# A row of RMS factors: made by TensorE transposes, or by a write to DRAM and a broadcast read

## The reference

```python
def rmsnorm(x, g):
    return x * lax.rsqrt(jnp.mean(x * x, axis=-1, keepdims=True) + EPS) * g

x = x + mixed @ w_o                      # mixed: gated sum of a convolution and a windowed attention
h2 = rmsnorm(x, mlp_norm_g)
x = x + jnp.square(jax.nn.relu(h2 @ w_up)) @ w_down      # w_up 1024x4096, w_down 4096x1024
return rmsnorm(x, final_norm_g)
```

## Time and profile before

| | |
|---|---|
| median of 3 runs | 763.24 us (763.02 to 763.28) |
| profiled execution | 763.45 us, of which the span from the first to the last instruction is 761.7 us |
| TensorE (matmul) busy | 752.7 us, 99% of the span |
| VectorE busy | 637.4 us, 84% |
| ScalarE busy | 407.6 us, 54% |
| GpSimd busy | 75.9 us, 10% |
| DMA | 128.13 MB, mean 168 GB/s |
| granted TensorE clock | 0.998 of full |

### The profile page before, as it was taken

The page is one execution under the profiler, slowest core; times in us unless marked ns, Lnnn a source line. Parts: engine busy times, 40 slices in busy tenths (PEclk is TensorE's granted clock), DMA queues, the critical chain, the costliest instruction groups (busy, mean ns, idle before and its releaser), DMA issues.

```text
span 761.7 us, 11518 instructions
## 1 busy us (share of the span) xinstructions
PE 752.7 (99%) x4563; PEld 675.0 (89%) x4563; DVE 637.4 (84%) x752; ACT 407.6 (54%) x529; POOL 75.9 (10%) x113
## 2 busy tenths in 40 slices
PE   8999999999999999999999999999999999999996
PEld 7888888888888999999988899889998999899985
DVE  5766688889896979886869899998799869986997
ACT  7424554453644655636616786654555356445565
POOL 3201000101112001010010101010101000010102
PEclk9999999999999999999999999999999999999999
DMA  7727313131219876779736866777676767777702
GB/s 255 244 83 278 111 55 111 56 111 55 72 39 262 242 186 169 194 237 327 235 80 198 219 160 173 174 205 177 175 209 172 215 166 190 196 184 203 194 1 111
DMA packets 70451, 128.13 MB, mean 168 GB/s; under 512 B 2620, under 2 KB 26244, under 8 KB 70404
## 3 DMA queue, kind: packets, MB, share of 16 engines
q1 hardware_dynamic: 53040, 85.23, 33.8%
q0 software_dynamic: 17152, 41.96, 25.4%
q10 hardware_dynamic: 212, 0.28, 0.1%
HBM read 121.14 MB, written 6.32 MB: 167 GB/s over the span
## 4 chain that ended last, share of the span: by engine, by line
PE 97%; DVE 1%; DMA 1%; ACT 0%; issue 0%; SPq 0%; ACTq 0%; DVEq 0%
PE pair L848 37%; PE pair L875 24%; PE pair L651 10%; PE pair L653 10%; PE pair L652 10%; PE pair L698 2%; PE pair L673 1%; PE pair L672 1%; PE pair L682 1%; DMA xn<-in_x 1%; PE pair L744 1%; PE pair L746 0%; PE pair L745 0%; PE pair L800 0%; DVE home_lo L1698 0%
## 5 line engine op out<-in xcount | busy, mean ns | idle before, releaser
L1164 ACT ACTIVATE high<-home_raw 128x2048 fp32r<-128x2048 f32 x84 | 160.9, 1916 | 156.2 <-PE pair L848 88.7
L1698 DVE TENSOR_TENSOR home_lo<-home_raw,high 128x2048 fp32r<-128x2048 f32 x84 | 192.2, 2288 | 35.3 <-ACT high L1164 34.7
L651 PE MATMUL pair<-h,wgt 128*128 128x512 f32 x320 | 126.7, 396 | 0.0
L653 PE MATMUL pair<-h,wgt 128*128 128x512 f32 x320 | 124.9, 390 | 0.0
L652 PE MATMUL pair<-h,wgt 128*128 128x512 f32 x320 | 124.8, 390 | 0.0
L653 PEld LDWEIGHTS pair<-h,wgt 128*128 128x128 f32 x320 | 60.1, 188 | 13.0
L652 PEld LDWEIGHTS pair<-h,wgt 128*128 128x128 f32 x320 | 60.3, 188 | 11.5
L651 PEld LDWEIGHTS pair<-h,wgt 128*128 128x128 f32 x320 | 60.2, 188 | 11.5
L875 PE MATMUL pair<-high,s_hi_tile 128*128 128x512 f32 x280 | 70.1, 391 | 0.0
L875 PE MATMUL pair<-home_lo,s_hi_tile 128*128 128x512 f32 x280 | 69.7, 390 | 0.0
L875 PE MATMUL pair<-high,s_lo_tile 128*128 128x512 f32 x280 | 69.7, 389 | 0.0
(11 more groups left out here) (222 smaller groups left out, 1151.8 us busy)
## 6 DMA issues: line engine op xcount, KB each, us to landing
raw<-in_w_in SPq DMA_DIRECT2D x42, 512.0 KB, 4.8
home_raw<-in_w_up SPq DMA_DIRECT2D x16, 1024.0 KB, 5.5
home_raw<-in_w_down SPq DMA_DIRECT2D x16, 1024.0 KB, 5.1
home_raw<-in_w_up POOLq DMA_DIRECT2D x12, 1024.0 KB, 8.4
home_raw<-in_w_down POOLq DMA_DIRECT2D x12, 1024.0 KB, 8.5
home_raw<-in_w_conv_out SPq DMA_DIRECT2D x4, 1024.0 KB, 8.2
home_raw<-in_w_attn_out SPq DMA_DIRECT2D x4, 1024.0 KB, 5.2
home_raw<-in_w_in SPq DMA_DIRECT2D x4, 1024.0 KB, 5.4
```

Source lines behind the costliest of these rows:

```text
L651: mm(bank[j][:, :], wh, rhs[:, 0, k, :], start=(k == 0), stop=False)
L653: last = mm(bank[j][:, :], wl, rhs[:, 0, k, :], start=False, stop=(k == KT - 1))
L1164: a(high[n % 2][:, :], home_raw[home_of(s, name)][:, :], ACT.Copy).then_inc(m_hi, 1)
L1698: v.tensor_tensor(home_lo[home][:, :], home_raw[home][:, :], f32(high[n % 2][:, :]), ALU.subtract).then_inc(m_lo, 1)
```

## The change

- VectorE no longer copies the factors to `rbc`, and TensorE no longer transposes it. PSUM bank 7 isn't used for this, and the wait of product N2 in stage 5 is gone.
- The reciprocals `rr2[:, 1, :]` are written to a tensor in DRAM, `factors_row`, by a DMA on ScalarE's queue: 128 partitions with 4 values each, so 128 pieces of 16 bytes. ScalarE waits until this has landed and then issues the read: 512 values, 2 KB, to each of 128 partitions, in the tile `rraw`. In memory the order is token-in-block first, block second, so ScalarE's copy from `rraw` to `rrow` puts it in order by reading with a stride of 4 values.
- `token_sums` stands one place earlier in VectorE's list, ahead of `low_part(4, M6)`, and `token_factors` ahead of `h2_low(M5)`. The root on ScalarE stands ahead of `high_part(4, M5)`. The write is issued behind that, the read behind `h2_high(M7)`.
- POOL waits for the read (`rrow_in`) before it issues the adding load T3 of stage 5.

```diff
@@ POOL
             for s in range(STAGES):
+                if s == 5:
+                    pool.wait_ge(rrow_in, 16)
                 pool.wait_ge(b12_in, 16 * (s + 1))
                 pool.dma_start(home_rows(home_of(s, "T3")), weights(s, 1, 1), accum_op=ALU.add).then_inc(t3_in, 16)
@@ PE
-            def row_transposes():
-                pe.wait_ge(rbc_ready, 1)
-                pe.wait_ge(h2_raw, 12)
-                for b in range(TB):
-                    last = nc.tensor.transpose(bank[7][:, b * P:(b + 1) * P], rbc[:, b, :], ident[:, :])
-                last.then_inc(rrow_t, 1)
...
-                    up_product(s, M5, True, between=(0, row_transposes) if s == 4 else None)
+                    up_product(s, M5, True)
...
-                if s == 5:
-                    pe.wait_ge(rrow_ready, 1)
                 product(s, N2, s < 6)
@@ ACT
                     h2_high(M5)
+                    act.wait_ge(rr2_step, 1)
+                    a(rr2[:, 0, :], ss2[:, 2, :], ACT.Sqrt, bias=eps[:, :], scale=1.0 / D).then_inc(rr2_step, 1)
                 high_part(s, M5)
                 if first:
-                    act.wait_ge(rr2_step, 1)
-                    a(rr2[:, 0, :], ss2[:, 2, :], ACT.Sqrt, bias=eps[:, :], scale=1.0 / D).then_inc(rr2_step, 1)
-                if first:
+                    act.wait_ge(rr2_step, 3)
+                    act.dma_start(factors_row[:, :], rr2[:, 1, :]).then_inc(row_out, 16)
                     h2_high(M7)
+                    act.wait_ge(row_out, 16)
+                    act.dma_start(rraw[:, :], bass.AP(factors_row[:, :].tensor, 0, [[0, P], [1, T]])).then_inc(rrow_in, 16)
                 else:
                     square(s, 0)
                 high_part(s, M7)
                 copy_out(s, zc12, M6, -1.0)
                 if first:
-                    act.wait_ge(rrow_t, 1)
-                    a(rrow[:, :], bank[7], ACT.Copy).then_inc(rrow_ready, 1)
+                    act.wait_ge(rrow_in, 16)
+                    a(rrow[:, :].rearrange("p (b n) -> p b n", b=TB), rraw[:, :].rearrange("p (n b) -> p b n", b=TB),
+                      ACT.Copy).then_inc(rrow_ready, 1)
@@ DVE
                 v.reciprocal(rr2[:, 1, :], rr2[:, 0, :]).then_inc(rr2_step, 1)
-                dve.wait_ge(rr2_step, 3)
-                v.tensor_copy(rbc[:, :, :], rr2[:, 1, :].rearrange("p (b n) -> p b n", n=1).to_broadcast([P, TB, P])
-                              ).then_inc(rbc_ready, 1)
...
             h2_low(M6)
+            token_sums()
             low_part(4, M6)
-            token_sums()
+            token_factors()
             h2_low(M5)
-            token_factors()
             low_part(4, M5)
```

More of the change, by code:

```diff
@@ L239, in build @@
         ty = place("ty", [P, 2, T])
-        rbc = place("rbc", [P, TB, P], offset=ty_at + 4 * T)
         zc11, zc12, zc22 = (place(n, [P, 4, 2 * P], offset=o) for n, o in
@@ L277, in build @@
         rrow = place("rrow", [P, T], offset=rrow_at)
+        rraw = place("rraw", [P, T], offset=ty_at + 4 * T)
         vdif = place("vdif", [P, TB - 1, KV * HD], offset=rrow_at)
@@ L295, in build @@
         h_sums = nc.dram_tensor("h_sums", (4, 2, P, 8 * P), F32)
+        factors_row = nc.dram_tensor("factors_row", (P, TB), F32)
         pair = [ctx.enter_context(nc.psum_tensor(f"pair{i}", [P, 2, T], F32)) for i in range(4)]
@@ L338, in build @@
         h2_sums, h2_split, h2_ready = sem("h2_sums"), sem("h2_split"), sem("h2_ready")
-        ss2_ready, rr2_step, rbc_ready = sem("ss2_ready"), sem("rr2_step"), sem("rbc_ready")
-        rrow_t, rrow_ready = sem("rrow_t"), sem("rrow_ready")
+        ss2_ready, rr2_step = sem("ss2_ready"), sem("rr2_step")
+        row_out, rrow_in, rrow_ready = sem("row_out"), sem("rrow_in"), sem("rrow_ready")
         b11_in, b22_in = sem("b11_in"), sem("b22_in")
```

## The result

The changed kernel takes 767.67 us (median of 6 runs, 766.73 to 768.82), the kernel before 763.05 us on the same chip (762.71 to 763.28). The ratio is 1.0061, with a 95% interval of 1.0050 to 1.0071: slower by 4.6 us, where 1.0 was predicted, and 0.8 us above the range.

The account below looks back on a forecast made before the run. TensorE, 97% of the chain, was taken to bound the kernel. T2's lateness of 1.67 less 0.66 slack gave +1.01, swallowing the 0.44 gain; 761.7 + 1.01 + 1.75 = 764.46, adjusted to the median: 764.2 us, range 762.6 to 766.9.

Parts of the forecast that it names:

- TensorE's gain: Four transposes of the broadcast factors leave TensorE's chain with nothing replacing them: -0.44 us by themselves.
- VectorE's and ScalarE's lists: Moved sums, reciprocal and root cause no stall; ScalarE's 2.08 us idle covers the write's wait; strided copy stays near 0.59 us.
- The row's time: Write to DRAM lands in 2.8 us, read in 2.6 us; the row is in SBUF at 461.1 us.
- my upper bound of 3.1: Longest landing allowed for the row's read: 2.5 us fixed plus 0.64 for 0.26 MB.
- the row's own bounds: Row in SBUF between 459.7 and 462.9 us, from the bounds of write and read.
- The estimate that the prediction works out from the Trainium skill: Each transfer about 2.0 us fixed plus bytes at 436 GB/s; both 4.6 us, row at about 460.3.
- The adding load: T3 (B22 added to B12, stage 5) issued 3.0 us late, lands in 8.3; VectorE's sum T2 starts 1.67 us late.
- the sign of sharing: T3 landing more than 9 us after its issue would show it sharing the DMA engines.
- rival 2: T3 shares DMA engines with SyncE's B21 load, taking 2.6 us more; TensorE loses 3.6 us: 766.9 us; chance 0.12.
- The slack: Least slack in VectorE's late queue is 0.66 us, at sum s1 of stage 5; TensorE's end moves +1.01 us.
- Rival 3: Write 3.9 us, read 3.1; row at 462.9, T3 at 471.45, TensorE +2.8: 766.0 us; chance 0.24 including cases down to +1.5.

Follow-up runs that it names:

- e8: Kernel before without the four transposes of the broadcast factors and without ScalarE's wait for them (factors not the tokens'): 762.55 us against 763.02.
- e5: Kernel before, with T3 of stage 5 also waiting for ScalarE's conversion of M7's weights in stage 4, no row transfer: 764.34 us against 763.02.
- e3: Changed kernel, with SyncE's load of B21 for stage 5 issued only when T3 has landed: 766.87 us against 763.11.
- e2: Kernel before, with only T3 of stage 5 made to wait, for rrow, and no transfer of a row: 768.06 us against 763.11.
- e13: Changed kernel without GpSimd's wait, SyncE issuing the 16-byte write and the read behind B21, first relu, square and rounding of stage 4 later: 765.59 us.
- e4: Changed kernel with 28 unused transposes of the identity matrix filling TensorE's gap in M3 of stage 4: 767.33 us against 763.11.
- e10: Changed kernel, the read taking 128 different 2 KB pieces of another DRAM tensor (factors not the tokens'): 767.82 us against 763.26.
- e1: Changed kernel without GpSimd's wait for the row's read ahead of T3: 764.53 us against 763.11.

## Why the prediction was wrong

**TensorE's gain.** 0.44 us, right: e8 measured 0.47, with the interval given above.

**VectorE's and ScalarE's lists.** Right. token_sums, the root, the reciprocal and the first relu came without a stall of note, and ScalarE's 1.97 us of idle time before M7's conversion hid the wait for the write. The copy's time doubled, where I had chosen no change; it hid too. The stride is the likely reason, and not SBUF: the squaring pass of ScalarE over 128x512 values in SBUF, without a stride, takes 0.63 us (line 1301 of before).

**The row's time.** The write was right, 2.8 us. The read was mis-sized: 3.7 us against 2.6, outside my upper bound of 3.1. The row came at about 462.0 in the times of before and not at 461.1, still inside the row's own bounds (459.7 to 462.9). The fault lies in the read's upper bound: I had added up a fixed part from large loads and the bytes at full rate, with nothing for packets that all read one place or for a slow start behind the small write. The estimate that the prediction works out from the Trainium skill (DMA: Bandwidth & Descriptors, Anatomy of one DMA), 4.6 us for both transfers, was further off: they took 6.5. The 256 KB stores' 2.1 us, which I said agree with it, are 0.5 us under the 2.6 that it gives for them.

**The adding load.** That it waits, that VectorE waits for it and what is queued behind, was right. Its duration is the step that failed: 8.3 us assumed, 10.3 measured, beyond the 9 us that I had named as the sign of sharing. I took 8.3 us from before, and set sharing with B21 (rival 2) aside for two stage 6 rows, from which I read "the one that moves first goes first". What they showed was only that a plain load starts late behind an adding one. B21, issued at 463.96 in after, moved its first packets after 467.5, and then took every second packet. In e5 T3 was issued 1.2 us earlier than in after, B21 started at the same point, T3 had nearly finished by then, and T3 took 8.6 us. The rule of the Trainium skill (DMA: Bandwidth & Descriptors, Queues, rings and completion order), round-robin between the queues with work, agrees with the 16 and 16 packets above; where I placed it beside the stage 6 rows, it was right and I was not. When a queue's first packets come is another matter, and that is what the stage 6 rows showed. Sharing is 0.9 us of T3's excess (after against e3, 10.3 and 9.4). The other 1.1 us are the one late part of T3's 16; that the fetch of instructions makes it late is likely and not shown.

**The slack.** The number 0.66 us at s1 was right where the lateness was 1.68 us (e5). At 4.57 us it would still be the place that costs most, 4.57 - 0.66 = 3.9 us, if the clock held. But the gap then comes first at an earlier place, the remainder of M3's weights. Its slack is 1.78 us (before: written by 472.57, read from 474.35), less the 0.44 us by which TensorE is early: 4.57 - 1.78 + 0.44 = 3.2 us of lateness, as measured. The fall of the clock behind this gap adds 1.59 and so brings TensorE past s1: 4.57 - 1.78 + 1.59 = 4.4 us. The prediction didn't count with the clock at all; it put that term at nothing.

**The miss in parts.** The row's lateness alone (T3 issued at 462.26, landing in 8.3 us) would have given 765.2 us by the prediction's own sum, inside the range. T3's further 2.0 us make it 767.2, the clock's share beyond s1, 4.4 - 3.9, some 767.6; measured were 767.67.

**The rivals.** Rival 2, with a chance of 0.12, named the mechanism and the place, and its 766.9 us are near the measured 767.7. That its figure is so near is luck in part: it took 2.6 us of sharing with the row on time, while sharing measured 0.9 and the late row, the late part of T3 and the clock made up the rest. Rival 3 named the slow read, together with a slow write that didn't come. The row came 0.9 us sooner than it said (462.0 against 462.9) and T3 still landed 1.1 us later (472.5 against 471.45). The effects add: a read 1.1 us late moves T3 into B21's time and that of the fetch. I had priced them one at a time.

## What to carry to other kernels

A wait put on a queue of loads costs what the delayed load then meets, and not the delay alone: price the load in its new place, against the transfers of that time, and ask when the next queue's packets come. When a gap on TensorE becomes likely, add what the clock takes behind it, and look for the next slack that this uses up. An instruction that fills another's wait isn't free to be moved, even when its own result is needed late.

## What was not expected of the hardware

A plain 1 MB load issued 2.3 us behind an adding one landed in 10.0 us instead of 5.0. One of the 16 parts of a transfer landed about 1.0 us behind the other fifteen (0.96 us in after, 1.06 in e3, 1.13 in e2), and the transfer with it. A write of 2 KB in 512 pieces of 4 bytes landed in 8.7 and 10.0 us, with some 5 us in which no DMA engine showed work and nothing landed; in 128 pieces of 16 bytes ahead of T3 in 2.7 to 3.1 us, and behind B21 (e13) in 5.4. Packets of 2 KB that all read the same 2 KB of DRAM held an engine for 0.14 to 0.15 us each (after, e3, e4), packets from different places for 0.085 (e10). ScalarE's copy with a stride of 16 bytes took 1.12 to 1.17 us, against 0.59 for the one without. TensorE idle for 3.1 us was followed by a stretch at the clock's lower level that cost 1.6 us. Idle for 2.35 us in e3 it was followed by such a stretch too (0.50 in 478 to 480); for 1.47 us in e1 it wasn't (1.00 in 472 to 476).
